# Products of 104 to 128 streamed columns in the inverse of a chunked gated DeltaNet

## What is computed

```python
def chunk_gated_delta(q, k, v, g, beta):
    ...
    a_mat = jnp.where(strict, jnp.einsum("bhnid,bhnjd->bhnij", kb, k) * decay, 0.0)
    eye = jnp.eye(c, dtype=q.dtype)
    rhs = jnp.concatenate([v * beta[..., None], kb * jnp.exp(gc)[..., None]], axis=-1)
    sol = lax.linalg.triangular_solve(a_mat + eye, rhs, left_side=True, lower=True,
                                      unit_diagonal=True)
    u, w = sol[..., :dv], sol[..., dv:]
    ...
    def step(s, inp):
        u_n, w_n, qk_n, qd_n, kt_n, gt_n = inp
        v_new = u_n - jnp.einsum("bhck,bhkv->bhcv", w_n, s)
        o = jnp.einsum("bhck,bhkv->bhcv", qd_n, s) + jnp.einsum("bhcj,bhjv->bhcv", qk_n, v_new)
        s = s * gt_n[..., None, None] + jnp.einsum("bhck,bhcv->bhkv", kt_n, v_new)
        return s, o
```

## Time and profile before

| | us |
|---|---|
| median of 3 runs (2744.5 to 2749.4) | 2747.4 |
| the profiled execution | 2753.1 |
| its span | 2751.4 |
| TensorE busy in the span | 2567.5 (93%) |
| VectorE, ScalarE, GpSimd busy | 1814.9, 1252.3, 1214.7 |
| mean granted clock of TensorE | 0.967 |

### The profile page before, as it was taken

One profiled execution on the slowest core, in us unless ns is written; L12 is line 12 of the kernel. 1 busy time (PEld: TensorE's weight loads), 2 busy tenths in 40 slices (PEclk: granted clock), 3 DMA queues, 4 the chain that ended last, 5 costly groups with the idle time before them and its releaser, 6 DMA issues. The chain is left out here.

```text
span 2751.4 us, 49312 instructions
## 1 busy us (share of the span) xinstructions
PE 2567.5 (93%) x18313; PEld 2484.3 (90%) x18313; DVE 1814.9 (66%) x2723; ACT 1252.3 (46%) x2169; POOL 1214.7 (44%) x1111
## 2 busy tenths in 40 slices
PE   6999999988986999999999699999999999999995
PEld 6999999988984899999999699999999998998994
DVE  5477777777006788888888667777777777676103
ACT  4466666663013534445443344554545545465102
POOL 1333333436241255554445354545555555573320
PEclk8999999999998999999999789999999999999997
DMA  5122122123104356544554542424244242423113
GB/s 157 47 61 61 61 61 61 61 86 116 46 17 158 86 151 168 161 142 124 140 159 143 166 128 50 120 50 114 59 108 121 58 112 53 113 71 111 50 35 123
DMA packets 243087, 268.95 MB, mean 98 GB/s; under 512 B 86747, under 2 KB 210220, under 8 KB 241276
## 3 DMA queue, kind: packets, MB, share of 16 engines
q1 hardware_dynamic: 242940, 266.96, 33.7%
HBM read 182.59 MB, written 84.33 MB: 97 GB/s over the span
## 5 line engine op out<-in xcount | busy, mean ns | idle before, releaser
L688 PE MATMUL ps<-dn_yhi,dn_whi 128*128 128x348 f32 x1128 | 385.0, 341 | 8.1 <-ACT p_vrow L1588 5.3
L2321 ACT ACTIVATE zz<-ps 104x416 fp32r<-104x416 f32 x560 | 282.7, 516 | 223.0 <-PE ps L2157 221.3
L689 PE MATMUL ps<-dn_ylo,dn_whi 128*128 128x348 f32 x1128 | 362.8, 322 | 0.0
L690 PE MATMUL ps<-dn_yhi,dn_wlo 128*128 128x348 f32 x1128 | 362.8, 322 | 0.0
L2444 DVE TENSOR_TENSOR pp<-ps,level_mask 104x416 fp32r<-104x416 f32 x480 | 275.7, 588 | 129.9 <-PE ps L2157 128.4
L688 PE MATMUL ps<-rg_yhi,rg_whi 128*128 128x348 f32 x912 | 295.8, 324 | 15.1 <-POOL rg_ylo_r L865 6.3
L689 PE MATMUL ps<-rg_ylo_r,rg_whi 128*128 128x348 f32 x912 | 295.3, 324 | 0.0
L690 PE MATMUL ps<-rg_yhi,rg_wlo 128*128 128x348 f32 x912 | 295.2, 324 | 0.0
L2159 PE MATMUL ps<-pp,zz 104*104 104x208 f32 x1440 | 265.7, 295 | 20.8 <-DVE pp L2444 11.9
L2159 PE MATMUL ps<-zz,pp 104*104 104x208 f32 x1440 | 247.0, 282 | 0.0
L688 PEld LDWEIGHTS ps<-dn_yhi,dn_whi 128*128 128x128 f32 x1128 | 212.9, 189 | 13.1 <-issue 9.6
(11 more groups left out here) (362 smaller groups left out, 7100.6 us busy)
## 6 DMA issues: line engine op xcount, KB each, us to landing
c_nq<-nq_scratch SPq DMA_DIRECT2D x160, 169.0 KB
dn_raw<-in_dn_w_in SPq DMA_DIRECT2D x48, 512.0 KB, 4.1
qd<-rows_scratch SPq DMA_DIRECT2D x160, 104.0 KB, 3.2
rg_raw<-in_rg_w_in SPq DMA_DIRECT2D x32, 512.0 KB, 4.5
nq_scratch<-p_nq SPq DMA_DIRECT2D x48, 338.0 KB
p_ex<-rows_scratch SPq DMA_DIRECT2D x32, 422.5 KB
nq_scratch<-p_rn SPq DMA_DIRECT2D x32, 338.0 KB
n_h<-h_scratch SPq DMA_DIRECT2D x16, 520.0 KB, 8.1
```

What stands on the lines that cost most here:

```text
L688: e.matmul(o, whi, mhi[:, t0:t0 + tn], start=(first and k == 0), stop=False)
L689: e.matmul(o, whi, mlo[:, t0:t0 + tn], start=False, stop=False)
L690: ins = e.matmul(o, wlo, mhi[:, t0:t0 + tn], start=False, stop=(last and k == end))
L2321: e.activation(zz[:, b, :, :], ps[0:CH, 2 * b + 1, 0:m4], ACT.Copy).then_inc(zev.sem, 1)
```

## The change

All products of the inverse but the fp32 ones now go from m = 0 to m = 3, and each streams 128 adjoining columns: the 104 of matrix m and the 24 that follow in memory, which are the first columns of matrix m + 1. They are written to the columns m x 104 to m x 104 + 128 of the bank; what falls into matrix m + 1's place is overwritten by its own product. For m = 3 the 24 extra columns have to exist behind the buffer. So zz, uu and the two halves of pp are laid behind each other in one tensor (`lane`, named inverse), with a spare strip of 24 at its end, and nhr and twos get such strips too. GpSimd fills uu and the strips once, at the start of the stage, and TensorE waits for that once. The fp32 products of level 8 only change their order.

```diff
-        nhr = sb(s, "nhr", [CH, 4, 4, CH], F32R)
-        uu, zz = sb(s, "uu", [CH, 2, 4, CH], F32R), sb(s, "zz", [CH, 2, 4, CH], F32R)
-        pp = sb(s, "pp", [CH, 2, 2, 4, CH], F32R)
-        twos = sb(s, "twos", [CH, 2, 4 * CH + 2], F32R)
+        WIDE = 128
+        SET = 4 * CH
+        lane = sb(s, "inverse", [CH, 2, 3 * SET + 3 * CH + WIDE], F32R)
+        zz, uu = (lane[:, :, k * SET:(k + 1) * SET].rearrange("p b (m i) -> p b m i", m=4) for k in (0, 1))
+        pp = lane[:, :, 2 * SET:4 * SET].rearrange("p b (c m i) -> p b c m i", c=2, m=4)
+        nh_rows, twos = sb(s, "nhr", [CH, 4, 3 * CH + WIDE], F32R), sb(s, "twos", [CH, 2, 3 * CH + WIDE], F32R)
+        nhr = nh_rows[:, :, 0:SET].rearrange("p b (m i) -> p b m i", m=4)
...
+            for b in range(2):
+                e.tensor_copy(uu[:, b, :, :], eye).then_inc(spare_done, 1)
+                e.tensor_copy(lane[:, b, 4 * SET:], c["ident"][0:CH, 0:WIDE - CH]).then_inc(spare_done, 1)
+            for rows, n in ((nh_rows, 4), (twos, 2)):
+                e.tensor_copy(rows[:, :, SET:], c["ident"][0:CH, 0:WIDE - CH].unsqueeze(1)
+                              .to_broadcast([CH, n, WIDE - CH])).then_inc(spare_done, 1)
...
-            MS = (3, 2, 1, 0)
-
-            def widened(bank, m, lhs, rhs):
-
-
-                if m == 0:
-                    return e.matmul(ps[0:CH, bank, 0:CH], lhs, rhs, start=True, stop=True)
-                o = ps[0:CH, bank, (m - 1) * CH:(m + 1) * CH].rearrange("p (a i) -> p a i", a=2)
-                return e.matmul(o, lhs, rhs.unsqueeze(1).to_broadcast([CH, 2, CH]), start=True, stop=True)
+            e.wait_ge(spare_done, 6)
+
+            def widened(bank, m, lhs, rows):
+                v = slice(m * CH, min(m * CH + WIDE, rows.shape[-1]))
+                return e.matmul(ps[0:CH, bank, v], lhs, rows[:, v], start=True, stop=True)
...
                     elif l <= LEVELS:
-                        old, p_ = zz[:, b], pp[:, b, (l - 1) % 2]
+                        at = (2 + (l - 1) % 2) * SET
                         e.wait_ge(yev.sem, yev.at(n, nth(g, l - 2, YS)))
                         e.wait_ge(zev.sem, zev.at(n, nth(g, l - 2, LEVELS)))
-                        for m in MS:
-                            ins = widened(2 * b, m, old[:, m, :], p_[:, m, :])
+                        for m in range(4):
+                            ins = widened(2 * b, m, zz[:, b, m, :], lane[:, b, at:])
                         ins.then_inc(ym.sem, 1)
-                        for m in MS:
-                            ins = widened(2 * b + 1, m, p_[:, m, :], old[:, m, :])
+                        for m in range(4):
+                            ins = widened(2 * b + 1, m, pp[:, b, (l - 1) % 2, m, :], lane[:, b, :])
                         ins.then_inc(zm.sem, 1)
...
```

More of the change, by code:

```diff
@@ L1903, in dn_chunks @@
                                          (("zeroed", 0), ("half", 1), ("squared", 2), ("summed", 2)))
+        spare_done = s.semaphore("dn_spare")
         block = s.block()
@@ L2171, in inverse @@
                             e.wait_ge(yev.sem, yev.at(n, nth(g - 2, YS - 1, YS)))
-                        for m in MS:
-                            ins = widened(2 * b, m, nhr[:, q4, m, :], two(b, m))
+                        for m in range(4):
+                            ins = widened(2 * b, m, nhr[:, q4, m, :], twos[:, b])
                         ins.then_inc(ym.sem, 1)
@@ L2176, in inverse @@
                             e.wait_ge(tb_done.sem, tb_done.at(n, g - 1))
-                        for m in MS:
-                            ins = widened(2 * b + 1, m, two(b, m), nhr[:, q4, m, :])
+                        for m in range(4):
+                            ins = widened(2 * b + 1, m, two(b, m), nh_rows[:, q4])
                         ins.then_inc(zm.sem, 1)
                     elif l <= LEVELS:
-                        old, p_ = zz[:, b], pp[:, b, (l - 1) % 2]
+                        at = (2 + (l - 1) % 2) * SET
                         e.wait_ge(yev.sem, yev.at(n, nth(g, l - 2, YS)))
                         e.wait_ge(zev.sem, zev.at(n, nth(g, l - 2, LEVELS)))
-                        for m in MS:
-                            ins = widened(2 * b, m, old[:, m, :], p_[:, m, :])
+                        for m in range(4):
+                            ins = widened(2 * b, m, zz[:, b, m, :], lane[:, b, at:])
                         ins.then_inc(ym.sem, 1)
-                        for m in MS:
-                            ins = widened(2 * b + 1, m, p_[:, m, :], old[:, m, :])
+                        for m in range(4):
+                            ins = widened(2 * b + 1, m, pp[:, b, (l - 1) % 2, m, :], lane[:, b, :])
                         ins.then_inc(zm.sem, 1)
@@ L2199, in inverse @@
                         e.wait_ge(u_done.sem, u_done.at(n, g + 1))
-                        for m in MS:
-                            ins = widened(2 * b + 1, m, pp[:, b, (LEVELS + 1) % 2, m, :], uu[:, b, m, :])
+                        for m in range(4):
+                            ins = widened(2 * b + 1, m, pp[:, b, (LEVELS + 1) % 2, m, :], lane[:, b, SET:])
                         ins.then_inc(zm.sem, 1)
```

2 lines of the change are left out of this document (1 added, 1 removed).

## The result

The changed kernel takes 2831.3 us (median of 4 runs, 2829.4 to 2833.4) against 2747.5 before: a ratio of 1.0289, 95% interval 1.0265 to 1.0314. It is slower by 84 us; 2802 was forecast, with a range of 2748 to 2858. The profiled execution has a span of 2829.2 us, 77.8 above that of before.

What follows compares the result with a forecast made beforehand. TensorE was taken to bound the only stage touched, 1569 to 2499 us. Clock losses of 75 us less a 20 us gain gave +55 us on a median of 2747.4: 2802 us, range 2748 to 2858.

Steps and rivals of the forecast that it cites:

- The saving at the high level: Groups of four products at the high clock take 0.36 us instead of 0.384; net gain 20 us (12 to 35).
- the start, two periods: At the stage's start the clock stays low until the fp32 run that began at 1613.52; +11 us.
- the two present falls: Low stretches at 1875.47 and 2339.68, at starts of heads, last until the long fp32 run; +11 each, +22 us.
- waits for ScalarE: Behind three of seven waits of 1.14 us the clock newly falls, +8 us each; +24 us (0 to 56).
- starts of heads with 0.73 us: Behind one or two of four VectorE waits the clock newly falls, +12 us each; +18 us (0 to 48).
- all else, the faster groups: Some 1000 groups at the high level save 0.024 us each, less up to 4 us lost at waits; -20 us.
- the run that was named: L2229, L2194 and L2238 together, the period's longest fp32 work; the first lasting rise was expected behind it, near 1625 us.
- The price of a low microsecond: Throughout the stage, each us of work at the low clock level was priced at one us more than at the high.
- A: Rival: the clock does not care for columns, stage clock stays 0.97, full gain; 2722 us; chance 0.18.
- B: Rival: the start and the two present falls last longer, no new fall; +8, 2755 us; chance 0.12.
- D: Rival: a group's pace stays 0.384 us, held by neither columns nor loads, and the clock stays; 2747 us; chance 0.05.
- C: Rival: all eleven waits, for ScalarE and at starts of heads, bring a fall; +119, 2866 us; chance 0.07.

Runs made afterwards that it cites:

- load128: The changed kernel with 128 instead of 104 stationary columns loaded for the first three products of a group; 2896.0 us (one run).
- w104: The changed kernel with each product streaming only its own matrix's 104 columns, no strips filled, 416 a group; 2895.1 us, 1.0482 of before.
- w128_fill: The changed kernel with unread fp32 products in TensorE's waits for ScalarE and for VectorE at starts of heads; 2751.4 us, 0.9999 of before.
- w200: The changed kernel with the first three products of a group widened from 128 to 200 columns, 728 a group; 2738.9 us, 0.9949 of before.

## Why the prediction was right

**The bound.** TensorE is the bound of the stage, before and after; its share of the span went from 93 to 94%. Right.

**The saving at the high level, term 20 us: too high.** The group was put at 0.36 us, 0.024 less than 0.384. Measured over four groups it is 0.375 against 0.388, 0.0125 less, and over a period 0.015 less. Even the upper end of 0.368, from the fp32 row of 0.092 us, was a little low, and half the low pace (0.087) was never reached; the choice of a value between the two was the error. load128 showed that the mechanism, the load as the bound, was right. At the low level the pace is unchanged, as forecast: 1749.33 to 1752.14 in the profile after are four groups in 2.81 us, 0.70 each, the first with its change of kind in it.

**The terms, measured.** The periods can be laid beside each other, before and after, 39 of them from the first products of nhr (1569.08 and 1566.00) to the last period's (2475.88 and 2554.13):

| term | forecast, us | measured, us |
|---|---|---|
| the start, two periods | +11 | +7.7 |
| the two present falls | +22 | +15.1 (7.8 and 7.4) |
| waits for ScalarE | +24, three of 8 | +34.8, six of 2.9 to 7.2 |
| starts of heads with 0.73 us | +18, one or two of 12 | +34.8, three of 11.0 to 12.7 |
| all else, the faster groups | -20 | -11.1, 26 periods |
| sum | +55 | +81.3 |

Each measured term is a difference of whole periods and so holds their faster groups too. The spans differ by 77.8 us, since what stands ahead of the stage was 3.1 us shorter.

The prices of the new falls were nearly right; those of the present falls and of the start were too high. The term that was mis-sized is the number of new falls, "three of seven" and "one or two" of four: there are six and three. I took a little under half for want of a row that tells how near the waits were to a fall. That the sum came as near as it did owes something to luck: the start and the present falls were put 10 us too high, which made up for a part of the missing falls.

The first lasting rise came at 1616.84, forecast near 1625, behind L2222, a slot earlier than the run that was named; two of the eleven later low stretches ended behind L2222 too, and not in such a run. The stage's clock is 0.87 (1569 to 2580 us), forecast 0.89.

**The price of a low microsecond.** The work at the low level went from 47 us (10.24 + 6.83 + 6.83 and 23 of the first stretch) to 256 (48 and 208), where 210 were forecast: 209 us more. Half of that, less 12 for the faster groups, would be 92 us, and 81 were measured. So such a microsecond costs less than the half that the prediction took. For a group it does: 0.69 us at the low level for 0.375 at the high one is 0.46 of it. Between kernels it is the same: w104 has 136 more than after and takes 64 us more (0.47), w128_fill 174 less and takes 80 less (0.46).

**The rivals.** A, the clock doesn't care for columns, fell: w200 and after differ in columns alone and by 92 us. The rule named beside it, of the Trainium skill, page "TensorE: Matmul & The Clock Gate", section "Loop structure matters more than you think", is that matmuls which follow at once stay warm and long waits make them cold. The trace disagrees: the clock falls behind a wait of 1.20 us, and in the low stretches of after the products follow at once for 24 us without its coming back. B and D fell with the number of falls and with the pace. C, all eleven waits, at 2866 us, came as near as the forecast did: there are eleven falls behind the start, where C had thirteen and the forecast six or seven; its time was 35 us too high, the forecast's 29 too low.

## What to carry to other kernels

Where the load of the stationary matrix bounds a product, columns streamed beyond the useful ones are free up to the load's time (a period takes 22.42 us with 416 or 512 columns a group), and they can be worth keeping for the clock: look at the granted clock by stretches, and at what stands ahead of every fall and rise, before taking them out. Waits that cost 1 us each can cost 6 to 12 more if the clock falls behind them, so price a change of TensorE's work by what the low level adds around the waits. Before you give an engine a higher clock, look at what its next waits are for: where a DMA holds them up, as at the start of this stage, the clock buys next to nothing. And 200 adjoining columns are better here than 128 or 104, and 0.5% faster than before.

## What the runs showed of the hardware that was not expected

Sixteen float32r products of 104 loaded columns take 1.51 us with 200 streamed columns in three of four, and 1.50 with 128 in all: 42% more columns for 1% more time. The clock fell in w104 behind waits of 0.33 us (1856.48) in groups of 416 columns, while with 728 it stayed high behind seven waits of 1.20 us. And thirteen fp32 products ahead of the stage lifted the clock within 4 us of their start (1561.04 to 1564.99), which the groups of the inverse didn't do in 16 us without a gap (1573 to 1589 us, before).
